# Sample attention in four column strips, between the prompt tiles of a decoder step

## The reference

```python
def cross_attend(hn, k, v, w_q, w_o):
    nb, t, _ = hn.shape
    q = (hn @ w_q).reshape(nb, t, MEM_HEADS, MEM_HEAD_DIM)
    s = jnp.einsum('nthd,nmhd->nhtm', q, k.astype(q.dtype), preferred_element_type=jnp.float32) * MEM_HEAD_DIM ** -0.5
    p = jax.nn.softmax(s, axis=-1).astype(hn.dtype)
    o = jnp.einsum('nhtm,nmhd->nthd', p, v.astype(hn.dtype))
    return o.reshape(nb, t, MEM_WIDTH) @ w_o
```

## Time and profile before

| | |
|---|---|
| timed runs | 2600.5, 2604.77 and 2605.12 us, median 2604.77 |
| profiled execution, first to last instruction (its span, the one time shown for it) | 2601.5 us |
| TensorE matmul busy | 2545.1 us, 98% of the span |
| TensorE weight load busy | 2515.1 us, 97% |
| VectorE, ScalarE, GpSimd busy | 1230.8, 637.5, 166.2 us |
| mean granted TensorE clock | 0.983 |

### The profile page before, as it was taken

The page is one execution under the profiler, slowest core; times in us unless marked ns, Lnnn a source line. Parts: engine busy times, 40 slices in busy tenths (PEclk is TensorE's granted clock), DMA queues, the critical chain, the costliest instruction groups (busy, mean ns, idle before and its releaser), DMA issues.

```text
span 2601.5 us, 47845 instructions
## 1 busy us (share of the span) xinstructions
PE 2545.1 (98%) x19828; PEld 2515.1 (97%) x19828; DVE 1230.8 (47%) x2028; ACT 637.5 (25%) x859; POOL 166.2 (6%) x189
## 2 busy tenths in 40 slices
PE   7999999999999999999999999999999999999997
PEld 7999999999999989999999999999999999999997
DVE  8724544546433426554345533554245533554346
ACT  7332222223223314222112221222112221222123
POOL 5000101000111002000000000000000000000004
PEclk9999999999999979999999999999999999999998
DMA  6332323232522312222222222322222222322223
GB/s 245 119 117 79 120 67 120 76 111 76 215 89 89 130 22 84 88 97 90 85 87 82 98 90 75 98 82 90 90 82 82 98 90 74 98 82 90 90 82 114
DMA packets 69593, 252.90 MB, mean 97 GB/s; under 512 B 8488, under 2 KB 12920, under 8 KB 68112
## 3 DMA queue, kind: packets, MB, share of 16 engines
q1 hardware_dynamic: 64144, 224.21, 26.2%
q0 software_dynamic: 5248, 25.71, 2.9%
HBM read 240.80 MB, written 9.09 MB: 96 GB/s over the span
## 4 chain that ended last, share of the span: by engine, by line
PE 92%; DVE 4%; POOL 1%; issue 1%; ACT 1%; DMA 1%; SPq 0%; POOLq 0%; DVEq 0%; ACTq 0%
PE ps_out L901 88%; PE ps_out L1117 1%; DVE a_lo L1227 1%; DVE w_lo L1219 1%; POOL sq_sum L594 1%; DVE x_t L1689 1%; PE ps_a L1083 1%; PE ps_a L1005 0%; ACT w_hi L616 0%; POOL sq_sum L493 0%; DMA out_conv_s<-pe 0%; DVE a_lo L1225 0%; DMA x_t<-in_x 0%; DMA m_raw<-in_mem 0%; ACT prob L798 0%
## 5 line engine op out<-in xcount | busy, mean ns | idle before, releaser
L901 PE MATMUL ps_out<-a_hi,w_hi 128*128 128x272 f32 x4704 | 979.6, 290 | 11.1 <-issue 7.4
L901 PE MATMUL ps_out<-a_hi,w_lo 128*128 128x272 f32 x4704 | 975.1, 289 | 1.4 <-issue 1.4
L901 PE MATMUL ps_out<-a_lo,w_hi 128*128 128x272 f32 x4704 | 973.5, 288 | 0.0
L901 PEld LDWEIGHTS ps_out<-a_hi,w_hi 128*128 128x128 f32 x4704 | 742.4, 189 | 16.8 <-issue 12.0
L901 PEld LDWEIGHTS ps_out<-a_lo,w_hi 128*128 128x128 f32 x4704 | 742.8, 189 | 0.0
L901 PEld LDWEIGHTS ps_out<-a_hi,w_lo 128*128 128x128 f32 x4704 | 738.0, 190 | 1.6 <-issue 1.6
L616 ACT ACTIVATE w_hi<-w_raw 128x1024 fp32r<-128x1024 f32 x402 | 411.6, 1051 | 758.3 <-PE ps_out L901 750.8
L1219 DVE TENSOR_TENSOR w_lo<-w_raw,w_hi 128x1024 fp32r<-128x1024 f32 x402 | 486.0, 1240 | 134.6 <-ACT w_hi L616 123.3
L1254 DVE TENSOR_TENSOR x_t<-ps_out,x_t 128x544 f32<-128x544 f32 (+1 forms) x112 | 81.1, 724 | 412.6 <-PE ps_out L901 403.0
L901 PE MATMUL ps_out<-h_hi,w_hi 128*128 128x272 f32 x1280 | 265.1, 288 | 1.2 <-DVE x_t L1254 0.8
L901 PE MATMUL ps_out<-h_hi,w_lo 128*128 128x272 f32 x1280 | 264.3, 288 | 0.0
(11 more groups left out here) (308 smaller groups left out, 1618.7 us busy)
## 6 DMA issues: line engine op xcount, KB each, us to landing
w_raw<-in_wall SPq DMA_DIRECT2D x406, 512.0 KB, 3.6
x_t<-in_x SPq DMA_DIRECT2D x4, 1088.0 KB, 7.7
x_t<-in_x POOLq DMA_DIRECT2D x4, 1088.0 KB, 10.0
kc_t<-in_k_cache POOLq DMA_DIRECT2D x1, 4096.0 KB, 24.0
vc_t<-in_v_cache POOLq DMA_DIRECT2D x1, 4096.0 KB, 12.5
out_y<-x_t SPq DMA_DIRECT2D x7, 544.0 KB, 3.0
rows<-gate_rows POOLq DMA_DIRECT2D x4, 816.0 KB, 7.7
m_raw<-in_mem SPq DMA_DIRECT2D x4, 512.0 KB, 7.5
```

The source lines that it names most:

```text
L901: ins_ = nc.tensor.matmul(out_bank(o, k)[:, 0:n[1]], w, a[:, c, m:m + n[1]], start=first and t == 0, stop=last and t == 2)
```

## The change

The sample tokens are no longer a fifth tile. Their scores (`scores_s`) are computed right after the first two prompt tiles' scores, with the sequences in the outer loop and the heads in the inner one, and each head writes its own 32 rows of one PSUM tile of 128 rows, that is, it uses its own 32 columns of the array. One maximum, one exponential, one sum and one division then serve all four heads on 128 rows. Two transposes (`turn_s`) turn the probabilities, VectorE spreads them into the zeroed tile `p_pad`, and in `value_s` the probabilities are the stationary operand (32 columns, again a strip for each head) and the cached values the moving one (128 columns): still 64 matmuls. ScalarE copies the result (`o_tok`), one transpose turns it back (`ps_sflip`), and `o_hi` and `o_lo` of the samples are taken from there. The two halves of `q_pad` are cleared earlier, in other places, and filled by 4 copies. GpSimd clears `p_pad` where the cached keys stood.

```diff
-        q_pad = [at("q_pad0", R_AL - 2 * NB * NS * 4, [P, 2, NB, NS]), at("q_pad1", R_RAW - 2 * NB * NS * 4, [P, 2, NB, NS])]
+        R_PAD = [R_SQA, R_RAW - 2 * NB * NS * 4]
+        assert 2 * NB * NS * 4 <= T * 4
+        q_pad = [at(f"q_pad{k}", R_PAD[k], [P, 2, NB * NS]) for k in range(2)]
+        s_mem = Place(at, [(R_Y, R_Y + NB * H * NM * 4)])
+        p_pad = s_mem.take("p_pad", [P, MT * H, NB * (NS + NT)])
+        prob_s = s_mem.take("prob_s", [P, NM])
+        o_tok = s_mem.take("o_tok", [P, P])
+        s_top, s_neg, s_sum, s_inv = [s_mem.take(f"s_{n}", [P, 1]) for n in ("top", "neg", "sum", "inv")]
...
+        ps_sscore = ps_out[:, 2 * last_q + 1, 0:NM]
+        ps_sturn, ps_svalue, ps_sflip = ps_a[:, 0, 0:MT * P], ps_a[:, 1, 0:P], ps_a[:, 1, P:2 * P]
...
+            nc.gpsimd.memset(q_pad[1][:, :, :], 0.0).then_inc(pad_zero, 1)
             squares(S_CROSS, T)
+            pool.wait_ge(ssq, S_CROSS + 1)
+            nc.gpsimd.memset(q_pad[0][:, :, :], 0.0).then_inc(pad_zero, 1)
             pool.wait_ge(half_used, 2 * U_O)
-            for pad in q_pad:
-                nc.gpsimd.memset(pad[:, :, :, :], 0.0).then_inc(pad_zero, 1)
             pool.dma_start(vc_t[:, :, :, :], ins["v_cache"]).then_inc(vc_in, 16)
-            pool.wait_ge(attended, CH + 1)
+            pool.wait_ge(s_scored, 1)
+            nc.gpsimd.memset(p_pad[:, :, :], 0.0).then_inc(p_zero, 1)
+            pool.wait_ge(attended, CH)
...
+            def exps_s():
+                act.wait_ge(s_topped, 1)
+                nc.scalar.activation(prob_s[:, :], ps_sscore, ACT.Exp, bias=s_neg[:, :], scale=SCALE,
+                                     accum_out=s_sum[:, :]).then_inc(s_exped, 1)
...
+                if i == 0:
+                    exps_s()
+                if i + 2 < CH:
...
+                if i == CH - 1:
+                    act.wait_ge(s_attended, 1)
+                    nc.scalar.activation(o_tok[:, :], ps_svalue, ACT.Copy).then_inc(s_copied, 1)
...
+            act.wait_ge(s_flipped, 1)
+            nc.scalar.activation(o_hi[:, :, SEQ:T], ps_sflip.rearrange("p (h t) -> p h t", h=H), ACT.Copy)\
+                .then_inc(s_hi_done, 1)
...
+            def scores_s():
+                pe.wait_ge(pad_ready, 1)
+                pe.wait_ge(kc_in, 16)
+                for b in range(NB):
                     for h in range(H):
-                        if i == 0 and h == H - 1:
-                            pe.wait_ge(evacuated, O_Q + H)
-                        m = nc.tensor.matmul(bank[:, h // 2, h % 2 * NM:(h % 2 + 1) * NM], q_t[:, h, P * i:P * i + P],
-                                             mk_t[:, h, :], start=True, stop=True)
-                else:
-                    pe.wait_ge(pad_ready, 1)
-                    pe.wait_ge(kc_in, 16)
-                    for h in range(H):
-                        for b in range(NB):
-                            m = nc.tensor.matmul(bank[0:NS, h // 2, h % 2 * NM:(h % 2 + 1) * NM], q_pad[h // 2][:, h % 2, b, :],
-                                                 kc_t[:, h, b, :], start=b == 0, stop=b == NB - 1)
-                m.then_inc(scored, 1)
+                        m = nc.tensor.matmul(ps_sscore[NS * h:NS * h + NS, :], q_pad[h // 2][:, h % 2, NS * b:NS * b + NS],
+                                             kc_t[:, h, b, :], start=b == 0, stop=b == NB - 1)
+                m.then_inc(s_scored, 1)
+            def turn_s():
+                pe.wait_ge(s_normed, 1)
+                for m in range(MT):
+                    t = nc.tensor.transpose(ps_sturn[:, P * m:P * m + P], prob_s[:, P * m:P * m + P], ident())
+                t.then_inc(s_turned, 1)
+            def value_s():
+                pe.wait_ge(s_padded, 1)
+                pe.wait_ge(vc_in, 16)
+                for b in range(NB):
+                    for m in range(MT):
+                        for h in range(H):
+                            v = nc.tensor.matmul(ps_svalue[NS * h:NS * h + NS, :],
+                                                 p_pad[:, m * H + h, NS * b:NS * b + NS], vc_t[:, b, m, P * h:P * h + P],
+                                                 start=b == 0 and m == 0, stop=b == NB - 1 and m == MT - 1)
+                v.then_inc(s_attended, 1)
             scores(0)
             scores(1)
-            for i in range(CH + 1):
-                r = P if i < CH else NS
+            scores_s()
+            for i in range(CH):
                 pe.wait_ge(normed, i + 1)
                 for h in range(H):
                     for m in range(MT):
                         n = h * MT + m
-                        t = nc.tensor.transpose(ps_b[:, n // 4, n % 4 * P:n % 4 * P + r],
-                                                prob[i % 2][0:r, h, P * m:P * m + P], ident(r))
+                        t = nc.tensor.transpose(ps_b[:, n // 4, n % 4 * P:n % 4 * P + P],
+                                                prob[i % 2][:, h, P * m:P * m + P], ident())
                 t.then_inc(turned, 1)
-                if i + 2 <= CH:
+                if i + 2 < CH:
                     scores(i + 2)
+                if i == CH - 1:
+                    value_s()
                 pe.wait_ge(turn_a, i + 1)
                 pe.wait_ge(turn_v, i + 1)
+                if i == 1:
+                    pe.wait_ge(s_exped, 1)
                 if i >= 2:
                     pe.wait_ge(o_lo_done, i - 1)
                 value = ps_value[i % 2]
-                if i < CH:
-                    for h in range(H):
-                        for m in range(MT):
-                            v = nc.tensor.matmul(value[:, h, :], mv_t[:, m, P * h:P * h + P],
-                                                 prob_t[i % 2][:, h * MT + m, :], start=m == 0, stop=m == MT - 1)
-                else:
-                    pe.wait_ge(vc_in, 16)
-                    for h in range(H):
-                        for b in range(NB):
-                            for m in range(MT):
-                                v = nc.tensor.matmul(value[:, h, NT * b:NT * b + NT], vc_t[:, b, m, P * h:P * h + P],
-                                                     prob_t[i % 2][:, h * MT + m, NT * b:NT * b + NT],
-                                                     start=m == 0, stop=m == MT - 1)
+                for h in range(H):
+                    for m in range(MT):
+                        v = nc.tensor.matmul(value[:, h, :], mv_t[:, m, P * h:P * h + P],
+                                             prob_t[i % 2][:, h * MT + m, :], start=m == 0, stop=m == MT - 1)
                 v.then_inc(attended, 1)
-            pe.wait_ge(o_hi_done, CH + 1)
-            pe.wait_ge(o_lo_done, CH + 1)
+                if i == CH - 2:
+                    turn_s()
+            pe.wait_ge(s_copied, 1)
+            nc.tensor.transpose(ps_sflip, o_tok[:, :], ident()).then_inc(s_flipped, 1)
+            pe.wait_ge(o_hi_done, CH)
+            pe.wait_ge(o_lo_done, CH)
+            pe.wait_ge(s_hi_done, 1)
+            pe.wait_ge(s_lo_done, 1)
...
+            dve.wait_ge(pad_zero, 2)
+            far = (NB - 1) * (NS + NT)
+            for k in range(2):
+                two = q_t[:, 2 * k:2 * k + 2, :]
+                copy(q_pad[k][:, :, 0:far].rearrange("p h (b x) -> p h b x", x=NS + NT)[:, :, :, 0:NT],
+                     two[:, :, SEQ:T - NT].rearrange("p h (b t) -> p h b t", t=NT))
+                m = copy(q_pad[k][:, :, far:far + NT], two[:, :, T - NT:T])
+            m.then_inc(pad_ready, 1)
             tops(0)
             tops(1)
             over_sum(0)
-            dve.wait_ge(pad_zero, 2)
-            for b in range(NB):
-                for k in range(2):
-                    m = copy(q_pad[k][:, :, b, NT * b:NT * b + NT], q_t[:, 2 * k:2 * k + 2, SEQ + NT * b:SEQ + NT * b + NT])
-            m.then_inc(pad_ready, 1)
-            for i in range(CH + 1):
-                r = P if i < CH else NS
+            dve.wait_ge(s_scored, 1)
+            link(nc.vector.tensor_reduce(s_top[:, :], ps_sscore, AX.X, ALU.max))
+            ts(s_neg[:, :], s_top[:, :], -SCALE, None, ALU.mult).then_inc(s_topped, 1)
+            for i in range(CH):
                 dve.wait_ge(turned, i + 1)
                 if i >= 2:
                     dve.wait_ge(attended, i - 1)
-                copy(prob_t[i % 2][:, 4:8, 0:r], b7.rearrange("p (n t) -> p n t", n=4)[:, :, 0:r]).then_inc(turn_v, 1)
-                if i + 1 <= CH:
+                copy(prob_t[i % 2][:, 4:8, :], b7.rearrange("p (n t) -> p n t", n=4)).then_inc(turn_v, 1)
+                if i + 1 < CH:
                     over_sum(i + 1)
-                if i + 2 <= CH:
+                if i == 1:
+                    dve.wait_ge(s_exped, 1)
+                    link(nc.vector.reciprocal(s_inv[:, :], s_sum[:, :]))
+                    ts(prob_s[:, :], prob_s[:, :], s_inv[:, :], None, ALU.mult).then_inc(s_normed, 1)
+                if i + 2 < CH:
                     tops(i + 2)
                 dve.wait_ge(o_hi_done, i + 1)
```

(64 more changed lines are left out.)

10 lines of the change are left out of this document (4 added, 6 removed).

## The result

The changed kernel takes 2568.4 us (median of 4 runs, 2565.4 to 2570.2) against 2603.8 of the kernel before beside it (2600.5 to 2605.1): ratio 0.9858, interval [0.9844, 0.9871]. It is faster by 35.5 us, 1.4%; forecast were 27.9. The profiled execution took 2569.7 us, its span 2568.2.

What follows compares the result with a forecast made beforehand. TensorE was taken to be on the cross-attention stage's path almost throughout. With two records at a time, +3.5 - 9.9 - 21.5 = -27.9 us from the median 2604.8 gave 2577, the clock terms cancelling; range 2568 to 2592.

Steps and rivals of the forecast that it cites:

- I take two: Sample scores and values: two records of neighbouring heads overlap, giving 6.9 us for each group and 2577 in all; chance 0.50.
- second rival: Sample scores and values: four records run at a time, one per head's strip; -34.8 us, 2570; chance 0.15.
- Sample scores into the first hole: After the second prompt scores, a 3.5 us hole: the moved scores delay the first transposes by 3.5 us, 0 by four.
- The middle: Sample scores gone from between third transposes and third values: gain 9.9 us, and a new TensorE hole of 4 us.
- Third values to W_o: From the third prompt values to the last projection: 35.7 us before, gain 21.5 us two at a time, 24.9 by four.
- Clock: W_o at full clock gains 2.6 us; a clock fall in the new 4 us hole costs 2.6; the two cancel.
- fourth rival: Clock stays low from the new hole through W_o, costing 11.6 us: -16.3 us, 2588; chance 0.06.
- third rival: Sample matmuls: a change of strip waits for the matmul before to end, 163 ns more a record; 2622; chance 0.04.
- the rule weighed there: Skill's rule on TensorE loads: a load overlaps matmuls in flight only where row groups differ; by it, the third rival.
- memset of p_pad: On POOL right after the sample scores: 2304 elements take 2.4 us, some 16 us before VectorE fills it.

Runs made afterwards that it cites:

- warm hole's kernel: Changed kernel plus fifteen matmuls that nobody reads, in TensorE's idle stretch ahead of the third values: 2564.2 us (one run).
- heads outermost: Changed kernel with the head loop outside, 16 records of a strip in a row in the scores and 32 in the values: 2585.9 us (one run).
- the strips that were not moved: Changed kernel's strips in the old order, sample scores between third transposes and values, sample values after the fourth: 2569.8 us, 0.9861 of the kernel before.

## Why the prediction was wrong, point by point

The kernel got faster by the steps forecast, but by more, and one step failed: **"I take two"**, with the reason that the second record of a head must wait for the first and that only it and the next head's first could run together. The waiting is true inside a strip; that it holds up the strips behind was the error, which a timeline in program order of one-strip work had no way to show. Four run together, 64 records in 3.66 us for the 6.9 of its sum, because a strip holds four records and program order moves on meanwhile (theory C). What happened is the second rival, given 0.15: 2570 for a measured 2568.4.

The steps of its sum, -34.8, each from the two timelines:
- *Sample scores into the first hole*, 0 by four: from the second scores to the first transposes 903.56 - 898.14 = 5.42 us for 5.19, +0.2. With two at a time it was to be +3.5.
- *The middle*, -9.9: from the first transposes to the third values 918.85 - 903.56 = 15.29 for 25.19; -9.9. The hole of 4 us is there, 4.02.
- *Third values to W_o*, -24.9 by four and -21.5 by two: 932.16 - 918.85 = 13.31 for 35.73, -22.4, and -25.0 without the 2.6 of the clock. In the warm hole's kernel, at full clock, it is 3.76 us from the third values to the sample values, for 3.8.
- *Clock*: the fall came where it was put, between 916 and 923, and cost 2.6; W_o got back 2.5 (5.57 - 3.09) of its 2.6. They cancel, as forecast. The fourth rival, a low clock up to W_o, did not happen.

Together +0.2 - 9.9 - 25.0 = -34.7; the median moved by 35.5. The third rival (a change of strip waits) is refuted by 3.66 us for 64 records that change strips every two. The 64 loads all go to the same rows, and at 110 ns each they would fill 7.0 us one after another; they are done within 3.66, under matmuls of other strips. So the rule weighed there does not hold for this case either. The memset of p_pad, put at 2.4 us (2304 elements at 0.5 per 512 make 2.25), took 2.01 and stayed hidden. The range's lower end was tied to the second rival's 2570 with 2 us to spare, though its chance was 0.15 and the medians move by up to 2.5 us between sets of runs (2603.8 to 2606.4 for the kernel before).

## What to carry to other kernels

Where small matmuls are given strips of the array, let the loop over strips be the inner one, and count how many records stand behind each other on one strip: here 4 in a row (two matmuls) were almost free, 8 cost more than twice the time and 16 to 32 three times or more. Before a term that rests on how many things overlap is put at a middle value, ask what order the evidence was taken in: a trace in which all such work has one strip says nothing for or against others. And a hole that a change opens on TensorE can be paid twice, by the wait (4.02 us here) and by the clock after it (2.6); work that is ready goes there.

## What the runs showed of the hardware

- A strip holds four records (or two matmuls), and strips overtake each other: with heads outermost, the second strip began after twelve of the first's 16. The Trainium skill, "TensorE: Matmul & The Clock Gate", Part 3, says that matmuls start and end in strict program order. The trace disagrees: by that order the scores of heads outermost would take some 13.2 us (61 x 0.216), and 11.50 was measured. In the changed kernel's own order it would be the forecast's 6.9 us if it held for each record, and 3.66 was measured; whole matmuls may keep their order there.
- Four strips gave 3.8 times, for 256 and for 128 columns alike (14.00 to 3.66, 14.16 to 3.70).
- An idle 3.30 us left the clock at 1.00 in the kernel before; 3.24 us at the same place, in the strips that were not moved, were followed by half rate. Why one and not the other stays open; so does what in the rest of the program moves the stage's start by up to 4 us (the second prompt scores begin between 895.00 and 899.03 in the changed kernel and its variants, which are alike up to there).
